# A two-block transformer on one core: delta-rule steps spread over the projections, and the pair products of two heads interleaved over row halves

## The reference

```python
def chunk_gated_delta_rule(q, k, v, g, beta):        # first block
    ...
    decay = jnp.exp(jnp.where(tril, gc[..., :, None] - gc[..., None, :], -jnp.inf))
    kb = k * beta[..., None]
    lower = jnp.where(strict, jnp.einsum('bnhid,bnhjd->bnhij', kb, k) * decay, 0.0)
    tmat = lax.linalg.triangular_solve(eye + lower, jnp.broadcast_to(eye, lower.shape), ...)
    u = tmat @ (v * beta[..., None])
    w = tmat @ (kb * jnp.exp(gc)[..., None])
    ...
    def step(state, inp):
        v_new = u_n - jnp.einsum('bhck,bhkv->bhcv', w_n, state)
        o_n = jnp.einsum('bhck,bhkv->bhcv', qd_n, state) + jnp.einsum('bhij,bhjv->bhiv', a_n, v_new)
        state = state * jnp.exp(gl_n)[..., None, None] + jnp.einsum('bhck,bhcv->bhkv', kd_n, v_new)
        return state, o_n

def gated_linear_attention(q, k, v, r, g_low, w_gate, b_gate, norm_g):   # second block
    log_a = jax.nn.log_sigmoid((g_low @ w_gate + b_gate).astype(jnp.float32)) / GLA_TAU
    ...
        b = jnp.cumsum(ab, axis=2)
        decay = jnp.exp(jnp.where(tril[:, :, None], b[:, :, :, None, :] - b[:, :, None, :, :], -jnp.inf))
        attn = jnp.einsum('bhid,bhjd,bhijd->bhij', qb, kb, decay)
```

## Time and profile before

| | us |
|---|---|
| median of 3 runs | 2552.22 (2548.5 to 2557.53) |
| profiled execution, its own time | 2556.78 |
| its span | 2555.0 |
| PE busy | 2315.3 |
| DVE busy | 835.6 |
| ACT busy | 528.7 |
| POOL busy | 54.5 |
| mean granted clock of PE | 0.948 |

### The profile page before, as it was taken

One profiled execution on the slowest core, in us unless ns is written; L12 is line 12 of the kernel. 1 busy time (PEld: TensorE's weight loads), 2 busy tenths in 40 slices (PEclk: granted clock), 3 DMA queues, 4 the chain that ended last, 5 costly groups with the idle time before them and its releaser, 6 DMA issues. The chain is left out here.

```text
span 2555.0 us, 34110 instructions
## 1 busy us (share of the span) xinstructions
PE 2315.3 (91%) x12870; PEld 1735.4 (68%) x12870; DVE 835.6 (33%) x1875; ACT 528.7 (21%) x1186; POOL 54.5 (2%) x28
## 2 busy tenths in 40 slices
PE   8898898887998889888699999999989989999998
PEld 6666765554775765544575777788877667787887
DVE  3364242223456323223335333211122532321112
ACT  2212321112312431110422422010012233201000
POOL 0120000000021000000000000000000000000000
PEclk9899989988989998999799999999999999999999
DMA  6221329996221044999544034433344404343333
GB/s 220 77 84 34 123 99 383 422 421 243 101 84 44 33 198 193 422 421 415 197 131 139 33 136 128 143 122 131 131 154 132 140 18 148 99 165 119 146 131 115
DMA packets 165154, 426.44 MB, mean 167 GB/s; under 512 B 40409, under 2 KB 54294, under 8 KB 140454
## 3 DMA queue, kind: packets, MB, share of 16 engines
...
...
## 5 line engine op out<-in xcount | busy, mean ns | idle before, releaser
L2005 PE MATMUL bank<-hT,W 128*128 128x256 f32 (+1 forms) x1440 | 330.2, 384 | 9.2 <-ACT b_gates L2147 5.9
L2005 PEld LDWEIGHTS bank<-hT,W 128*128 128x128 f32 (+1 forms) x1440 | 268.2, 190 | 56.6 <-issue 16.9
L259 PE MATMUL bank<-hT,W 128*128 128x272 f32 x928 | 250.1, 430 | 16.5 <-issue 11.6
L2993 PE MATMUL bank<-hT,W 128*128 128x256 f32 x1024 | 231.5, 388 | 13.7 <-issue 6.9
L259 PEld LDWEIGHTS bank<-hT,W 128*128 128x128 f32 x928 | 192.9, 211 | 64.6 <-issue 21.0
L3010 PE MATMUL bank<-u_hid,W 128*128 128x256 f32 x1024 | 225.1, 381 | 6.3 <-issue 6.3
L2993 PEld LDWEIGHTS bank<-hT,W 128*128 128x128 f32 x1024 | 197.8, 194 | 47.1 <-issue 19.9
L3010 PEld LDWEIGHTS bank<-u_hid,W 128*128 128x128 f32 x1024 | 193.5, 190 | 37.9 <-issue 12.6
L1398 PE MATMUL bank<-W,e_hs 128*32 128x256 f32 x2048 | 136.0, 425 | 35.4 <-DMA W<-in_w 27.0
L1318 PE MATMUL bank<-e_sel,rowsH 128*128 128x128 f32 (+1 forms) x768 | 153.4, 335 | 7.9 <-issue 7.9
L1318 PEld LDWEIGHTS bank<-e_sel,rowsH 128*128 128x128 f32 (+1 forms) x768 | 117.0, 209 | 46.7 <-issue 22.2
...
## 6 DMA issues: line engine op xcount, KB each, us to landing
W<-in_w SPq DMA_DIRECT2D x128, 1024.0 KB, 16.8
...
```

The costliest lines, as they stand in the source:

```text
L259: mm = nc.tensor.matmul(bank[:, 0:T], w[:, k, c0:c0 + P], m.hT[:, k, :], **st)
L2005: mm = nc.tensor.matmul(o[0:n, 0:S2], w[:, k, a:a + n], m.hT[:, k, :], start=(k == 0), stop=(k == KT - 1))
L2993: mm = nc.tensor.matmul(ps[j][:, 0:S2], w[:, k, j * P:(j + 1) * P], m.hT[:, k, :], start=(k == 0), stop=(k == KT - 1))
```

## The change

Two edits, which share no code. In the table of the delta rule, the first chunk starts at 66.5 instead of 62.0 and its steps lie 4.0 apart instead of 2.0 to 3.5; the second starts at 75.0 instead of 73.0. In `gated_linear`, the loop over level groups becomes the outer one and the two heads alternate within it, matmul by matmul, on PE; the products of the two heads go to two buffers, `prod` and `ex`, so that all four products come before the two reductions; ACT's Exp of the next unit, which overwrites `ex`, waits for a new semaphore `g_reduced` instead of `g_qk`; and the far products wait for `g_prod` in the new order of banks.

```diff
--- before.py
+++ after.py
@@ -334,8 +334,8 @@
     return on_sync, on_tensor, on_scalar, on_vector, on_gpsimd
 
 
-DELTA_START = (62.0, 73.0, 104.0)
-DELTA_STEPS = ((0.0, 2.0, 5.0, 8.0, 11.0, 3.5), (0.0, 4.0, 9.0, 14.0, 19.0, 9.0), (0.0, 4.0, 9.0, 14.0, 19.0, 9.0))
+DELTA_START = (66.5, 75.0, 104.0)
+DELTA_STEPS = ((0.0, 4.0, 8.0, 12.0, 16.0, 4.0), (0.0, 4.0, 9.0, 14.0, 19.0, 9.0), (0.0, 4.0, 9.0, 14.0, 19.0, 9.0))
 
 
 def delta_rule(nc, m, S, ctx):
@@ -2701,6 +2701,7 @@
     take = Room(room)
     la, ex, qs, ks = take(2, 256), take(8, P), take(8, P), take(8, P)
     prod = take(8, P)
+    pair = (prod, ex)
     far = take(2, 2, P)
     att = take(4, 3, P)
     t1 = ex.rearrange("p a b -> p (a b)")[:, 0:512].rearrange("p (t n) -> p t n", t=2)
@@ -2738,21 +2739,22 @@
             nc.tensor.matmul(B[0][:, :], lhs, m.sums[:, 0:4, :], start=True, stop=True)
             nc.tensor.matmul(B[1][:, 0:384], lhs, m.sums[:, 4:7, :], start=True, stop=True)
             nc.tensor.matmul(B[1][:, 384:512], lhs, m.sums[:, 7 + t, :], start=True, stop=True).then_inc(S["g_sums"], 1)
-            for a in range(2):
-                hs = slice(64 * a, 64 * a + 64)
-                for b in range(2):
-                    yield order(u, 3 + a + 0.3 * b)
-                    pe.wait_ge(S["g_qk"], u + 1)
-                    if (a, b) == (1, 1):
-                        pe.wait_ge(S["g_prod"], 4 * u + 1)
-                    for lv in range(4 * b, 4 * b + 4):
+            for b in range(2):
+                yield order(u, 3 + b)
+                pe.wait_ge(S["g_qk"], u + 1)
+                if b:
+                    pe.wait_ge(S["g_prod"], 4 * u + 1)
+                for lv in range(4 * b, 4 * b + 4):
+                    for a in range(2):
+                        hs = slice(64 * a, 64 * a + 64)
                         mm = nc.tensor.matmul(B[PAIR[a][b]][:, lv % 4 * P:(lv % 4 + 1) * P], ks[hs, lv, :], qs[hs, lv, :], start=True, stop=True)
-                    mm.then_inc(S["g_pairs"], 1)
+                        if lv % 4 == 3:
+                            mm.then_inc(S["g_pairs"], 1)
             if t == 1:
                 for a in range(2):
                     hs = slice(64 * a, 64 * a + 64)
                     yield order(u, 4.9 + 0.1 * a)
-                    pe.wait_ge(S["g_prod"], 4 * u + 2 + a)
+                    pe.wait_ge(S["g_prod"], 4 * u + 3 - a)
                     nc.tensor.matmul(B[a][:, 0:P], far[hs, f, 0, :], far[hs, f, 1, :], start=True, stop=True).then_inc(S["g_far"], 1)
         yield END
         pe.wait_ge(S["g_att"], 1)
@@ -2785,7 +2787,7 @@
             yield order(u, 1)
             act.wait_ge(S["g_sums"], u + 1)
             if u:
-                act.wait_ge(S["g_qk"], u)
+                act.wait_ge(S["g_reduced"], u)
             nc.scalar.activation(ex[:, 0:4, :], B[0][:, :].rearrange("p (l i) -> p l i", l=4), ACT.Exp, scale=1.0 / 16)
             nc.scalar.activation(ex[:, 4:8, :], B[1][:, :].rearrange("p (l i) -> p l i", l=4), ACT.Exp, scale=1.0 / 16)
             act.drain().then_inc(S["g_ex"], 1)
@@ -2845,15 +2847,17 @@
             nc.vector.tensor_copy(ks[:, 7, :], k)
             nc.vector.tensor_tensor(far[:, f, t, :], ex[:, 7, :], q if t else k, ALU.mult)
             dve.drain().then_inc(S["g_qk"], 1)
+            for b in range(2):
+                for a in range(2):
+                    yield order(u, 3.4 + b + 0.2 * a)
+                    dve.wait_ge(S["g_pairs"], 4 * u + 2 * b + a + 1)
+                    nc.vector.tensor_tensor(pair[a][:, 4 * b:4 * b + 4, :], B[PAIR[a][b]][:, :].rearrange("p (l i) -> p l i", l=4),
+                                            m.pairs[:, 4 * b:4 * b + 4, :], ALU.mult).then_inc(S["g_prod"], 1)
+            yield order(u, 4.8)
+            dve.drain()
             for a in range(2):
-                for b in range(2):
-                    yield order(u, 3.4 + a + 0.3 * b)
-                    dve.wait_ge(S["g_pairs"], 4 * u + 2 * a + b + 1)
-                    nc.vector.tensor_tensor(prod[:, 4 * b:4 * b + 4, :], B[PAIR[a][b]][:, :].rearrange("p (l i) -> p l i", l=4),
-                                            m.pairs[:, 4 * b:4 * b + 4, :], ALU.mult).then_inc(S["g_prod"], 1)
-                dve.drain()
-                nc.vector.tensor_reduce(att[:, 2 * f + a, t, :], prod[:, :, :].rearrange("p l i -> p i l"), AX.X, ALU.add)
-                dve.drain()
+                nc.vector.tensor_reduce(att[:, 2 * f + a, t, :], pair[a][:, :, :].rearrange("p l i -> p i l"), AX.X, ALU.add)
+            dve.drain().then_inc(S["g_reduced"], 1)
         yield END
         dve.wait_ge(S["g_far_sb"], 2)
         dve.drain().then_inc(S["g_att"], 1)
```

2 lines of the change are left out of this document (1 added, 1 removed).

## The result

The changed kernel takes 2535.43 us (median of 7 runs, 2522.59 to 2538.66) against 2553.14 us before (7 runs, 2548.5 to 2560.95): a ratio of 0.9924, 95% interval 0.9906 to 0.9942, so 17.7 us less, with the interval 15 to 24 us. The forecast was 2525.7, in a range of 2508 to 2546: the time lies inside the range, 9.7 us above the forecast, and two thirds of the forecast's gain of 26.5 us came. The profiled execution took 2522.59 us, the fastest of the seven, and the one before had taken 2556.78. The difference of these two, 34 us, must not be read as the change: most of what follows is about how much of it is.

The account below looks back on a forecast made before the run. PE, busy 91% of the span, was taken to bound the kernel. Per layer 7.25 us in the first block and 6.0 in the second gave 14.5 + 12.0 = 26.5 us for two layers, so 2525.7 us, range 2508 to 2546.

Parts of the forecast that it names:

- The starting waits of 5.05 us: First block, start of the 16-token chunk: four PE waits for DVE or ACT, 5.05 us per layer, get covered by projections.
- (a): First block: PE's L474 waits for 16-token steps queued on DVE behind top-k rounds, 0 to 3.3 us.
- (b): First block: POOL's rope slows DVE's L630 and L631, so PE's L450 waits, 0.35 to 2.9 us.
- The later end, 1.8 us of loss: First block, stage's later end: L926's wait grows by 1.5 us; smaller moves behind the start lose 0.3, per layer.
- The waits together, 1.75 us of gain: First block, per layer: starting waits of 5.05 us less 1.5 of new waits and 1.8 of later losses.
- The clock, 5.5 us: First block: projection products slowed by the half clock get faster, 5.5 us per layer, bounds 0 and 8.9.
- rival 4: Larger gain: 2.4 GHz throughout the first block's stretch, 8.9 us, few new waits, L2011 at full speed; 2510 us; chance 0.12.
- The second block, 6.0 us per layer: Gated branch: alternating products and DVE's new order bring L2285 5.2 us earlier, unit 3 adds 0.8.
- 1 (first block nothing): First block: spreading steps only moves waits and clock drops to the chunk's end, gaining nothing; 2540 us; chance 0.24.
- 2 (DVE bounds the branch): Gated branch: DVE's 6.6 us per unit stays, so faster PE groups gain nothing; 2538 us, reordering alone 2533; chance 0.15.
- 3 (slower): 16-token chunk's end holds PE: new waits and slow products cost 21.6 us per layer against 16.6 gained; 2562; chance 0.06.

Follow-up runs that it names:

- e6: Changed kernel with the first chunk's old steps, still started at 66.5: 2534.72 us, ratio 0.9936 to the kernel before.
- e7: Changed kernel with the first chunk's new steps but its old start at 62.0: 2551.22 us, ratio 0.9988 to the kernel before.
- e5: Changed kernel with the second chunk's start back at 73.0 instead of 75.0: 2527.69 us, ratio 0.9887 to the kernel before.
- e0: The changed kernel run again without any edit, for a second profile: 2533.54 us, ratio 0.9914 to the kernel before.
- e1: The kernel before with only the new delta rule table, second block as before: 2537.55 us, ratio 0.9939 to the kernel before.
- e2: Changed kernel with the old delta rule table, so only the gated edit: 2542.21 us, ratio 0.9952 to the kernel before.
- e3: Changed kernel with one head's four products behind one another instead of alternating heads: 2539.05 us, ratio 0.9941 to the kernel before.
- e10: New steps with the old start at 62.0, plus each POOL rope instruction split into four: 2536.41 us, ratio 0.9916 to the kernel before.

## Why the prediction was right, point by point

- *The starting waits of 5.05 us go.* They did, all four, and L430 of the third chunk stands at 159.28 (about 160 was forecast). e6 and e7 show what each half does: the waits at L436 and L459 stay with the old steps, the one at L430 with the old start.
- *New waits (a) and (b), 1.5 us.* Measured 2.25 and 0.91, 3.2 together: twice the term, within the bounds of 0.35 to 6.2. The mechanism is the one that was named (the rope over L630, L657 behind the rounds), except that L631 escaped it and L611, ahead of L630, was held as well. (The POOL row is not the one that L650 met at 153.00, as it ends at 152.80; that was L331, up to 155.44.) What the forecast missed is how near the cliff is: with the start 4.5 units earlier, three steps meet the rope instead of one, and the table's gain is lost (e7).
- *The later end, 1.8 us of loss.* L926's wait grew by 1.58 (1.5 forecast), and e5 takes it back.
- *The waits together, 1.75 us of gain.* Measured 1.7, by luck. The waits that the forecast named come to 5.05 - 3.2 - 1.6, about nothing. The rest came from the steps around the third chunk's start, for which it had 0.3 of loss: the waits at L450 (2.98), L436 (0.93) and before L754 (0.65) went, those at L466 (0.99) and L459 (1.25 to 2.99) came or grew.
- *The clock, 5.5 us.* PE's busy time per stage fell by 5.4 in the mean of twelve stages against four, so the term was right in the mean. It has a spread that the forecast did not name: 239.2 to 249.2 us with the new table, 243.9 to 250.7 with the old one. In the first profile 8.5 and 7.7 us went, in e0 7.1 and 4.6. That is also why the first profile shows rival 4's clock (0.98) while the median is far from rival 4's time.
- *The second block, 6.0 us per layer.* Measured 4.5, the same in both layers: the term that was mis-sized. Two steps of it failed. First, a unit's old products were priced as two groups of 16 at 2.05; the kernel before ran them as 8 and 24, and the change of row half inside the 24 already overlapped: in unit 0, 3.1 us now stand against 3.6, a gain of 0.5 and not 1.0. So L2361 came 4.6 us earlier and not 5.2. Second, the gain at L2361 was carried unchanged to L2285. From L2361's start to L2285 it is now 8.52 us instead of 7.59: L2366 waits 0.45 us for L2278, and L2373 starts 0.45 us later behind L2371 than it did, for a reason that the profile doesn't show. The two steps cost 0.6 and 0.9 us, which is the 1.5 that is missing. That L2278 is due 0.45 us later than DVE was not looked up.
- *The sum.* 14.5 + 12.0 was forecast; the stages show 14.2 + 9.0; the times 17.7 and 20.6 (e0), with an interval of 15 to 24 for the first. The medians, 2535.43 and 2533.54, lie at the upper edge of the forecast's own range (2517 to 2534), one just outside it. Of the 2.6 to 5.5 us between stages and times nothing is assigned to a stage; profiles that lie below their kernels' medians are enough to make it.
- *Rivals.* The total time lies between the forecast and the rivals at 2533, 2538 and 2540 and could not have told them apart. 1 (first block nothing) is excluded by e1 alone, faster by 10 to 21 us. 2 (DVE bounds the branch) is excluded as far as it says that PE's shorter groups only move waits: e2 gains 7 to 17 us, and e3 loses 2.0 and 3.4 us of stage without alternation. 3 (slower) did not happen here, but its mechanism is e7's: one POOL instruction for each small DVE step. Of the 10 to 13 us that e7's stages cost, e10 gives 5 to 6 to it.
